# Gate and up products by one level of Strassen's scheme, and a down projection in two parts

## The chip, the cores and the metric

The kernel runs on one core of a Trainium2 chip. The metric is the device time of one execution in microseconds, as the median of several runs.

## The reference

One encoder layer on 512 tokens with 2048 features. The attention part (two groups of eight heads, and an output projection) stands ahead of the change and is not touched. What the change concerns is the feed-forward part:

```python
h2 = rms_norm(x, norm2_g) * (1 + sc2[:, None]) + sh2[:, None]
ff = (silu(h2 @ w_gate) * (h2 @ w_up)) @ w_down     # 2048 -> 5632 -> 2048
x = x + g2[:, None] * ff
return rms_norm(x, final_g)
```

## The kernel before, in words

Everything lies with features on the 128 partitions and the 512 tokens in columns. X is 16 tiles of 128x512; the normed input h2 stands as two fp32r parts, H_hi and H_lo (its rounded value and the rest), of 16 tiles each. Each weight is brought in as fp32 into one of four `raw` slots (SP's queue, `load`), copied by ScalarE to its rounded part W_hi (`split` at L705) and subtracted by VectorE to its rest W_lo (`split` at L1040). A product of two such pairs takes three matmuls of 512 columns: hi by hi, hi by lo, lo by hi (`tile`, L435 to L437).

A "piece" is eight weight tiles of 128x128 (1024 columns of W_hi, 512 KB). One gate/up step f makes 128 of the 5632 rows of F: two pieces of w_gate into bank Pb[0], two of w_up into Pb[1], 96 matmuls; ScalarE takes silu of Pb[0] to `gate` (L1005), VectorE multiplies by Pb[1] to `ftile` (L1524), and the pair F_hi, F_lo is made of it at once (L1009, L1526). There are 44 such steps, in four chunks of FC = 11. After each chunk a down part runs over the 16 tiles of X: two pieces of six and five tiles of w_down by the chunk's 11 tiles of F into Tb[0] or Tb[1], then `update_x` (L1429) adds the result to X. In the last chunk GpSimd sums squares of X behind the updates; then the column norm and the output follow.

The order of each engine is written out by hand. The semaphores that matter: `lo_done` counts finished low parts of weights (TensorE waits for it at each piece, SP reloads a raw slot by it), `used` counts pieces that TensorE has finished (ScalarE waits for it before it overwrites a part of W_hi; there are two parts, so a split can be one piece ahead), `gated`, `f_made`, `f_hi` and `mlp_ready` order the steps around F, `x_new` counts updates of X.

Of the kernel before, what the change touches and what calls it, by code (L numbers as in the profile page):

```python
# [20 lines left out]
F32 = mybir.dt.float32  # L21
# [4 lines left out]
P = 128  # L26
# [15 lines left out]
DK = (6, 5)  # L42
EPS = 1e-6
# [18 lines left out]
CP = 4 * FC + 2 * KT  # L62
# [11 lines left out]
def layer(nc, x, c, w_ada, b_ada, norm1_g, w_first, w_in, rpb, na_g, lam_p, sub_g, t5, w_out, norm2_g, w_gu, w_down,  # L74
          final_g, out):
    ctx = ExitStack()
    with ctx:
# [9 lines left out]

        H_hi = sb("H_hi", KT * S, F32R)
# [9 lines left out]
        W2_lo = nc.alloc_sbuf_tensor_at("W2_lo", [P, PW], F32R, offset=raw_at + (RAW_B + 1) * PW * 4)  # L98
        sq = sb("sq", 2 * S)
# [26 lines left out]
        F_hi = nc.alloc_sbuf_tensor_at("F_hi", [P, FC * S], F32R, offset=overlay)  # L126
        F_lo = nc.alloc_sbuf_tensor_at("F_lo", [P, FC * S], F32R, offset=overlay + FC * S * 4)
# [22 lines left out]
        t5_d = nc.dram_tensor("t5_d", [NAH, 1024], F32, kind="Internal")  # L150
        keys_d = nc.dram_tensor("keys_d", [NK, P, S], F32, kind="Internal")
# [53 lines left out]
        gated, f_made, f_hi = sem("gated"), sem("f_made"), sem("f_hi")  # L205
        dve_passed, pool_passed = sem("dve_passed"), sem("pool_passed")
# [5 lines left out]
        def w_parts(slot):  # L212

            if slot < 2:
                return W_hi[:, slot * PW:slot * PW + PW], W_lo[:, slot * PW:slot * PW + PW]
            return W2_hi[:, :], W2_lo[:, :]

# [53 lines left out]
        def _(sp):  # L271
# [135 lines left out]
            def mlp_loads(cc, f0):  # L407
                n0 = CP * cc + MLP0
                with sp.Fori(f0, FC) as f:
                    for j in range(4):  # L410
                        sp.wait_ge(lo_done, n0 + 4 * f + (j - 3))
                        load(j, w_gu[bass.ds(cc * (4 * FC) + 4 * f + j, 1)].rearrange("a p n -> (a p) n"), PW)
                with sp.Fori(0, KT // 2) as m:
                    for j in range(4):
                        sp.wait_ge(lo_done, n0 + 4 * m + (4 * FC + j - 3))
                        src = w_down[bass.ds(cc * KT + 2 * m + j // 2, 1)].rearrange("a p n -> (a p) n")
                        k0 = DK[0] * P * (j % 2)
                        load(j, src[:, k0:k0 + DK[j % 2] * P], DK[j % 2] * P)

            mlp_loads(0, 1)  # L420
            with sp.Fori(1, CH) as cc:
                mlp_loads(cc, 0)
# [7 lines left out]
        def _(pe):  # L430
# [242 lines left out]
            def chunk(cc, peel):  # L673
                n0 = CP * cc + MLP0
                f0 = 0
                if peel:
                    pair(n0, Pb, lambda k: pe.wait_ge(mlp_ready, k + 1))
                    f0 = 1
                with pe.Fori(f0, FC) as f:
                    for g in gate_up(n0, f):  # L680

                        pe.wait_ge(f_made if g else gated, cc * FC + f)
                with pe.Fori(0, KT // 2) as i:
                    for b in range(2):
                        m = 2 * i + b
                        pe.wait_ge(x_new, cc * KT + m + (KT - 1))
                        for h in range(2):
                            pe.wait_ge(mlp_ready, cc * FC + (KT + (DK[0] if h == 0 else FC)))
                            piece(n0 + 2 * m + (4 * FC + h), h, Tb[b], F_hi, F_lo,
                                  range(DK[0] * h, DK[0] * h + DK[h]), FC - 1)  # L690

            chunk(0, True)
            with pe.Fori(1, CH) as cc:
                chunk(cc, False)
# [4 lines left out]
        def _(act):  # L699
# [53 lines left out]
            def col_root(n):  # L753

                act.activation(root_warm[:, :], eps[:, :], ACT.Sqrt)
                act.wait_ge(x_new, KT if n == 3 else KT * (CH + 1))
# [228 lines left out]
            def mlp_group(cc, q):  # L985

                return (CP // 4) * cc + q + (NH + KT // 2)

            def split_gu(cc, f, j, slot_free=2):
                split(CP * cc + MLP0 + 4 * f + j, j % 2, j, landings(j, mlp_group(cc, f)), slot_free=slot_free)  # L990

            def split_down(cc, i, j):
                split(CP * cc + MLP0 + 4 * i + (4 * FC + j), j % 2, j, landings(j, mlp_group(cc, i + FC)), DK[j % 2] * P)

            def gate_up(cc, f, nxt):
                n = CP * cc + MLP0 + 4 * f
                pair = isinstance(f, int) and f == 0
                if not pair:
                    split_gu(cc, f, 1)
                    split_gu(cc, f, 2)  # L1000
                    split_gu(cc, f, 3)
                else:
                    nxt()
                act.wait_ge(used, n + (3 if pair else 2))
                act.activation(gate, Pb[0][:, :], ACT.Silu).then_inc(gated, 1)  # L1005
                if not pair:
                    nxt()
                act.wait_ge(f_made, cc * FC + f + 1)
                act.activation(F_hi[:, bass.ds(f * S, S)], ftile, ACT.Copy).then_inc(f_hi, 1)  # L1009

            def down(cc, i, nxt):
                for j in range(1, 4):
                    split_down(cc, i, j)
                if nxt:
                    nxt()

            def chunk(cc, last_one, f0=0):
                if f0:
                    gate_up(cc, 0, lambda: split_gu(cc, 1, 0, 4))
                with act.Fori(f0, FC - 1) as f:  # L1020
                    gate_up(cc, f, lambda: split_gu(cc, f + 1, 0))
                gate_up(cc, FC - 1, lambda: split_down(cc, 0, 0))
                with act.Fori(0, KT // 2 - 1) as i:
                    down(cc, i, lambda: split_down(cc, i + 1, 0))
                down(cc, KT // 2 - 1, None if last_one else lambda: split_gu(cc + 1, 0, 0))

            chunk(0, False, 1)
            with act.Fori(1, CH - 1) as cc:
                chunk(cc, False)
            chunk(CH - 1, True)  # L1030
# [4 lines left out]
        def _(dve):  # L1035
# [478 lines left out]
            def gate_up(cc, f, last_one):  # L1514
                n = CP * cc + MLP0 + 4 * f
                t = cc * FC + f
                if not (isinstance(f, int) and f == 0):
                    for j in range(1, 4):
                        split(n + j, j % 2, j)
                split(n + 4, 0, 0, DK[0] * P if last_one else PW)  # L1520
                dve.wait_ge(gated, t + 1)
                dve.wait_ge(used, n + 4)
                dve.wait_ge(mlp_ready, t + KT)
# [5 lines left out]
            def down(cc, i, nxt):  # L1529
# [5 lines left out]
                if nxt:  # L1535
                    split(n + 4, 0, 0, nxt)
                update_x(2 * i + 1, Tb[1], 5 * KT, n + 4)

            def chunk(cc, last_one, f0=0):
                if f0:  # L1540
                    gate_up(cc, 0, False)
# [194 lines left out]
```

## Time and profile before

| | us |
|---|---|
| median of 3 runs | 2379.63 (2378.16 to 2379.69) |
| profiled execution, its own time | 2379.1 |
| span of its profile | 2377.4 |
| attention part, up to the first gate matmuls | about 922 |
| feed-forward part (gate, up, down) | about 922 to 2357 |
| norm and output at the end | 2357 to 2377 |

In the profile L435 stands for line 435 of the kernel. PE is TensorE's matmul stream and PEld its weight loads, DVE is VectorE, ACT ScalarE, POOL GpSimd, SP the queue that issues most DMAs. A group names what is written and read (P<-H_hi,W_hi), the shape, the count, the busy time, the mean of one record in ns and the idle time ahead of it with its releaser. Matmul records overlap: the time of one is longer than the distance between two.

### The profile page before, as it was taken

To read this page: it belongs to the slowest core of one execution; us is meant where nothing else is said; L and a number is where in the kernel's file an instruction comes from. 1 tells how busy PE (TensorE), PEld (TensorE's weight loads), DVE (VectorE), ACT (ScalarE), POOL (GpSimd) and SP (SyncE) were. 2 spreads that over 40 slices of the span, in tenths; PEclk is the share of its full clock that TensorE was granted. 3 is DMA by queue.
4 is the path that set the end of the run, shared out by engine and by line. 5 is a ranking of instruction groups with operands and counts; after the bars stand their busy time and mean duration, and the time that the engine had idled before them with its cause. 6 is when DMAs were issued, how large, how long until landed. Compare 5 with 4: busy or idle time off the path is not lost.

```text
span 2377.4 us, 29120 instructions
## 1 busy us (share of the span) xinstructions
PE 2318.9 (98%) x10280; PEld 1883.5 (79%) x10280; DVE 1162.3 (49%) x1590; ACT 693.5 (29%) x978; POOL 236.0 (10%) x211
## 2 busy tenths in 40 slices
PE   7999999999999998999999999999999999999997
PEld 4878888766777886888888888888888888888885
DVE  6877777776767897222333222333222233222234
ACT  4234333444444114222222222222222222222221
POOL 4012333100004330000000000000000000000032
PEclk9999999999999998999999999999999999999998
DMA  9896766433435882222233322233222233222233
GB/s 335 271 358 171 201 196 197 165 108 128 170 109 210 324 289 71 97 97 97 82 97 106 103 95 94 84 96 109 97 97 97 82 96 113 97 97 88 87 97 107
DMA packets 120058, 333.75 MB, mean 140 GB/s; under 512 B 11897, under 2 KB 36617, under 8 KB 119505
## 3 DMA queue, kind: packets, MB, share of 16 engines
q1 hardware_dynamic: 115282, 318.03, 39.7%
q0 software_dynamic: 3728, 15.01, 2.7%
q8 instruction: 21, 0.34, 0.1%
q10 hardware_dynamic: 1008, 0.21, 0.0%
q14 instruction: 19, 0.16, 0.0%
HBM read 325.55 MB, written 7.65 MB: 140 GB/s over the span
## 4 chain that ended last, share of the span: by engine, by line
PE 92%; DVE 4%; DMA 2%; ACT 1%; POOL 1%; issue 1%; DVEq 0%; ACTq 0%; POOLq 0%
PE P L435 19%; PE P L437 19%; PE P L436 19%; PE T L435 9%; PE T L437 9%; PE T L436 9%; DMA att<-in_w_ada 1%; PE T L498 1%; PE S L480 1%; DVE W_lo L1040 1%; PE O L510 1%; PE O L511 1%; PE S L481 1%; PE O L512 1%; PE S L482 1%
## 5 line engine op out<-in xcount | busy, mean ns | idle before, releaser
L435 PE MATMUL P<-H_hi,W_hi 128*128 128x512 f32 x2112 | 840.1, 398 | 20.8 <-POOL ident L1594 10.8
L1040 DVE TENSOR_TENSOR W_lo<-raw,W_hi 128x1024 fp32r<-128x1024 f32 (+2 forms) x416 | 473.6, 1138 | 726.0 <-ACT W_hi L705 722.6
L437 PE MATMUL P<-H_hi,W_lo 128*128 128x512 f32 x2112 | 825.4, 391 | 0.0
L436 PE MATMUL P<-H_lo,W_hi 128*128 128x512 f32 x2112 | 825.0, 391 | 0.0
L705 ACT ACTIVATE W_hi<-raw 128x1024 fp32r<-128x1024 f32 (+2 forms) x416 | 406.2, 977 | 1056.8 <-PE P L437 568.4
L435 PEld LDWEIGHTS P<-H_hi,W_hi 128*128 128x128 f32 x2112 | 398.0, 188 | 117.8 <-issue 18.3
L437 PEld LDWEIGHTS P<-H_hi,W_lo 128*128 128x128 f32 x2112 | 397.9, 188 | 84.4
L436 PEld LDWEIGHTS P<-H_lo,W_hi 128*128 128x128 f32 x2112 | 398.5, 189 | 80.5 <-issue 1.9
L435 PE MATMUL T<-F_hi,W_hi 128*128 128x512 f32 x704 | 273.9, 389 | 0.0
L436 PE MATMUL T<-F_lo,W_hi 128*128 128x512 f32 x704 | 273.9, 389 | 0.0
L437 PE MATMUL T<-F_hi,W_lo 128*128 128x512 f32 x704 | 273.9, 389 | 0.0
L1642 POOL TENSOR_TENSOR sq<-X 128x512 f32 (+1 forms) x38 | 62.3, 1639 | 1540.0 <-DVE X L1429 1489.6
L437 PEld LDWEIGHTS T<-F_hi,W_lo 128*128 128x128 f32 x704 | 132.2, 188 | 27.5
L435 PEld LDWEIGHTS T<-F_hi,W_hi 128*128 128x128 f32 x704 | 132.2, 188 | 27.4
L436 PEld LDWEIGHTS T<-F_lo,W_hi 128*128 128x128 f32 x704 | 132.2, 188 | 27.3
L1429 DVE SCALAR_TENSOR_TENSOR X<-T,mod,X 128x512 f32 (+1 forms) x78 | 58.6, 751 | 129.7 <-PE T L437 129.2
L1049 DVE CUSTOM_DVE_ANT_0 adar<-adar,csb 128x1024 f32<-128x1024 f32 x72 | 97.2, 1364 | 33.7 <-DMA adar<-in_w_ada 33.7
L1524 DVE TENSOR_TENSOR gf<-gf,P 128x512 f32<-128x512 f32 x44 | 30.3, 689 | 145.4 <-PE P L437 145.4
L435 PE MATMUL T<-H_hi,W_hi 128*128 128x512 f32 x256 | 99.8, 390 | 1.1 <-DVE W_lo L1040 0.7
L437 PE MATMUL T<-H_hi,W_lo 128*128 128x512 f32 x256 | 99.6, 389 | 0.0
L436 PE MATMUL T<-H_lo,W_hi 128*128 128x512 f32 x256 | 99.6, 389 | 0.0
L1009 ACT ACTIVATE F_hi<-gf 128x512 f32 (+1 forms) x44 | 27.8, 632 | 231.2 <-DVE gf L1524 231.2
(167 smaller groups left out, 1645.6 us busy)
## 6 DMA issues: line engine op xcount, KB each, us to landing
raw<-in_w_gu SPq DMA_DIRECT2D x176, 512.0 KB, 3.2
raw<-in_w_in SPq DMA_DIRECT2D x72, 512.0 KB, 4.3
adar<-in_w_ada SPq DMA_DIRECT2D x72, 512.0 KB, 4.3
att<-in_w_ada SPq DMA_DIRECT2D x32, 1024.0 KB, 10.6
att<-in_w_ada SPq DMA_DIRECT2D x56, 512.0 KB, 4.8
raw<-in_w_down SPq DMA_DIRECT2D x64, 384.0 KB, 3.0
raw<-in_w_down SPq DMA_DIRECT2D x64, 320.0 KB, 2.9
raw<-in_w_out SPq DMA_DIRECT2D x32, 512.0 KB, 4.9
```

The costliest lines, as they stand in the source:

```text
L435: pe.matmul(bank[:, :], wh, xh, start=start, stop=False)
L436: pe.matmul(bank[:, :], wh, xl, start=False, stop=False)
L437: return pe.matmul(bank[:, :], wl, xh, start=False, stop=stop)
L480: pe.matmul(Sb[t % 2][:, :], qh[r, cols], kh[r, :], start=True, stop=False)
L481: pe.matmul(Sb[t % 2][:, :], qh[r, cols], kl[r, :], start=False, stop=False)
L705: act.activation(w_parts(slot)[0][:, 0:cols], raw[:, raw_slot * PW:raw_slot * PW + cols], ACT.Copy).then_inc(hi_done, 1)
L1009: act.activation(F_hi[:, bass.ds(f * S, S)], ftile, ACT.Copy).then_inc(f_hi, 1)
L1040: dve.tensor_tensor(lo[:, 0:cols], raw[:, raw_slot * PW:raw_slot * PW + cols], hi[:, 0:cols].bitcast(F32), ALU.subtract).then_inc(lo_done, 1)
L1049: dve.tensor_tensor_reduce(wt, wt, csb[:, half * 1024:half * 1024 + 1024], 1.0, 0.0, ALU.mult, ALU.add, st[:, acc:acc + 1]).then_inc(count ...
L1429: dve.scalar_tensor_tensor(xm, bank[:, :], mod[:, bass.ds(m + g0, 1)], xm, ALU.mult, ALU.add)\
L1524: dve.tensor_tensor(ftile, gate, Pb[1][:, :], ALU.mult).then_inc(f_made, 1)
L1642: pool.tensor_tensor(sq[:, S:2 * S], xk, xk, ALU.mult).then_inc(pool_sq, 1)
```

## The change

Of the 44 gate/up steps the first NPL = 4 stay as they are. In the other 40 the product of the 256x2048 weight block (gate and up rows of one step) and the 2048x512 input is taken as a 2x2 by 2x2 block product: the weights are A11, A12 (gate, first and second half of the features) and A21, A22 (up), the input is B11, B12, B21, B22 (two halves of the features by two blocks of HS = 256 tokens). One level of Strassen's scheme in Winograd's form makes seven products ("forms") where there were eight:

- input sums, made once during steps 1 to 3 by VectorE with their high parts by ScalarE (`make_t`, `t_high_half`, `t_low`): T1 = B12 - B11, T3 = B22 - B12, T2 = B22 - T1, T4 = B21 - T2, as hi and lo pairs;
- weight sums, made in each set by VectorE in the raw slots (`add_raw`, four of 128x1024);
- seven forms of eight tiles, each split to high and low as pieces were, each of 24 matmuls with 256 columns, in five banks beside the two of before; form 5 accumulates on form 0's bank, after ScalarE has copied form 0 to `p1s`;
- the results put together by VectorE with five operations of 256 columns (u2, u3, u4 and both halves of ftile) and `c_12`; silu in two halves (`silu_11`, `silu_12`), and one product of 512 columns (`f_product`).

The places for parts of weights are W_hi/W_lo and the columns of H_hi/H_lo that hold B12, which is not needed once the T's are made. F is no longer split as it is made: GpSimd's queue stores each `ftile` to device memory (`store_f`), and loads runs of tiles back (`load_f`, F_RUNS) into the places of T1 to T3 and of H, where ScalarE and VectorE split them (`f_high`, `f_low`). The down projection runs in CD = 2 parts of 22 tiles of F instead of four of 11, two tiles of X at a time (`down_pair`) in alternating banks; its pieces keep six and five tiles. TensorE waits for single tiles of F (`f_ready`) in the first pair of each part.

The diff, cut to its core:

```diff
-            def gate_up(n0, f):
-                for g in range(2):
-                    yield g
-                    for h in range(2):
-                        piece(n0 + 4 * f + (2 * g + h), h, Pb[g], H_hi, H_lo, half_kts(h), KT - 1)
...
+            def form(f, i, bank, rhs, start=True, reopen=False):
+                pe.wait_ge(lo_done, form_no(f, i + 1))
+                wh, wl = form_parts(FORM_SLOT[i])
+                out = bank[:, 0:HS]
+                for j in range(HALF):
+                    hi, lo = [w[:, j // 2, (j % 2) * P:(j % 2) * P + P] for w in (wh, wl)]
+                    xh, xl = rhs[j]
+                    pe.matmul(out, hi, xh, start=start and j == 0, stop=False, skip_group_check=reopen)
+                    pe.matmul(out, hi, xl, start=False, stop=False, skip_group_check=reopen)
+                    mm = pe.matmul(out, lo, xh, start=False, stop=j == HALF - 1, skip_group_check=reopen)
+                mm.then_inc(used, 1)
+
+            def product_set(f, first=False):
+                pe.wait_ge(gated, NPL) if first else pe.wait_ge(gate_a, f - NPL)
+                form(f, 0, Pb[0], B11, reopen=True)
+                if first:
+                    pe.wait_ge(f_made, NPL)
+                    pe.wait_ge(t_lo, 4 * HALF)
+                else:
+                    pe.wait_ge(u_made, 5 * f - 5 * NPL)
+                form(f, 1, Pb[1], T4c)
+                form(f, 2, Sb[0], T3c)
+                form(f, 3, Sb[1], T1c)
+                form(f, 4, Tb[0], T2c)
+                pe.wait_ge(p1_kept, f - (NPL - 1))
+                form(f, 5, Pb[0], B21, start=False, reopen=True)
+                if not first:
+                    pe.wait_ge(c12_made, f - NPL)
+                form(f, 6, Tb[1], B22)
...
+            def down_pair(c, i, banks, banks_free, f_wait=False, by_row=False):
+                for q in range(8):
+                    p, b = down_piece(q, by_row)
+                    if p == 0:
+                        banks_free(b)
+                    t0 = FD * c + (0, DK[0], FC, FC + DK[0])[p]
+                    n = down_no(c, i, q)
+                    pe.wait_ge(lo_done, n + 1)
+                    wh, wl = w_parts(q % 2)
+                    for j in range(DK[p % 2]):
+                        t = t0 + j
+                        if f_wait and b == 0:
+                            pe.wait_ge(f_ready, t + 1)
...
+            def product_set(f, first=False):
+                if not first:
+                    split_loaded(f, 0, form_no(f, -2))
+                    silu_11(f - 1)
+                split_loaded(f, 1, form_no(f, 0 if first else -1))
+                split_form(f, 2, summed, 4 * f + (1 - 4 * NPL), form_no(f, 0))
+                if not first:
+                    silu_12(f - 1)
+                split_form(f, 3, summed, 4 * f + (2 - 4 * NPL), form_no(f, 0))
+                act.wait_ge(used, form_no(f, 1))
+                if not first:
+                    act.wait_ge(u_made, 5 * f - (5 * NPL + 4))
+                act.activation(p1s, Pb[0][:, 0:HS], ACT.Copy).then_inc(p1_kept, 1)
+                split_form(f, 4, summed, 4 * f + (3 - 4 * NPL), form_no(f, 1))
+                split_loaded(f, 5, form_no(f, 2))
+                split_form(f, 6, summed, 4 * f + (4 - 4 * NPL), form_no(f, 3))
...
+            def product_set(f, first=False):
+                g5 = 5 * f - 5 * NPL
+                if not first:
+                    split_form(f, 0)
+                dve.wait_ge(raw_in[2], landings(2, f + GRP0))
+                add_raw(0, 0, 2)
+                split_form(f, 1)
+                if not first:
+                    c_12(f - 1)
+                add_raw(2, 2, 3)
+                if not first:
+                    f_product(f - 1)
+                split_form(f, 2)
+                add_raw(3, 3, 0)
+                split_form(f, 3)
+                split_form(f, 4)
+                split_form(f, 5)
+                add_raw(1, 1, 3)
+                split_form(f, 6)
+                dve.wait_ge(used, form_no(f, 5))
+                dve.wait_ge(p1_kept, f - (NPL - 1))
+                dve.tensor_tensor(u2, Tb[0][:, 0:HS], p1s, ALU.subtract).then_inc(u_made, 1)
...
+            def c_12(f):
+                dve.wait_ge(used, form_no(f, 7))
+                dve.wait_ge(u_made, 5 * f - 5 * (NPL - 1))
+                dve.tensor_tensor(u4, Tb[1][:, 0:HS], u4, ALU.subtract).then_inc(c12_made, 1)
...
+            def silu_11(f):
+                act.wait_ge(used, form_no(f, 6))
...
+            split_down(0, 0, 0, slot_free=3)
+            silu_11(FT - 1)
+            f_high(0, 1, 2, 3)
+            split_down(0, 0, 1, slot_free=3)
+            f_high(4, 5)
+            silu_12(FT - 1)
+            f_high(6, 7)
...
+            def load_f(r, n_used):
+                t0, t1 = F_RUNS[r]
+                pool.wait_ge(used, n_used)
+                pool.wait_ge(f_stored, 16 * t1)
...
+            for r, n in enumerate((DOWN0 - 4, DOWN0 - 3, DOWN0 - 3, DOWN0 - 2, DOWN0, DOWN0, DOWN0)):
+                load_f(r, n)
...
+            for r, q in ((7, 2), (8, 2), (9, 4), (10, 4), (11, 6), (12, 6)):
+                load_f(r, down_no(0, HALF - 1, q))
```

## Rows read from the trace of the kernel before

**Rows 1.** The page: busy shares of the span, and granted clock in 40 slices.

```profile
PE 2318.9 (98%) x10280; PEld 1883.5 (79%) x10280; DVE 1162.3 (49%) x1590; ACT 693.5 (29%) x978; POOL 236.0 (10%) x211
...
PEclk9999999999999998999999999999999999999998
```

**Rows 2.** The page's chain of work that ended last.

```profile
PE 92%; DVE 4%; DMA 2%; ACT 1%; POOL 1%; issue 1%; DVEq 0%; ACTq 0%; POOLq 0%
PE P L435 19%; PE P L437 19%; PE P L436 19%; PE T L435 9%; PE T L437 9%; PE T L436 9%; DMA att<-in_w_ada 1%; PE T L498 1%; PE S L480 1%; DVE W_lo L1040 1%; PE O L510 1%; PE O L511 1%; PE S L481 1%; PE O L512 1%; PE S L482 1%
```

**Rows 3.** Grouped lines of 945 to 2367 us (columns as on the page).

```profile
L435 PE MATMUL P<-H_hi,W_hi 128*128 128x512 f32 x1373 | 534.1, 389 | 0.0
...
L1040 DVE TENSOR_TENSOR W_lo<-raw,W_hi 128x1024 fp32r<-128x1024 f32 (+2 forms) x299 | 323.3, 1081 | 691.1 <-ACT W_hi L705 688.1
L705 ACT ACTIVATE W_hi<-raw 128x1024 fp32r<-128x1024 f32 (+2 forms) x299 | 282.7, 945 | 849.2 <-PE P L437 484.1 <-PE T L437 365.2
...
L435 PEld LDWEIGHTS P<-H_hi,W_hi 128*128 128x128 f32 x1372 | 257.6, 188 | 53.4
```

**Rows 4.** Timeline, gate/up step: start, duration, engine, group.

```profile
1400.15 0.39 PE L436 MATMUL P<-H_lo,W_hi 128*128 128x512 f32 x1
...
1400.37 0.39 PE L437 MATMUL P<-H_hi,W_lo 128*128 128x512 f32 x1
1400.38 0.19 PEld L435 LDWEIGHTS P<-H_hi,W_hi 128*128 128x128 f32 x1
...
1401.28 0.39 PE L435 MATMUL P<-H_hi,W_hi 128*128 128x512 f32 x1
```

**Rows 5.** Timeline of VectorE, then of ScalarE, around one product.

```profile
1412.77 0.69 DVE L1526 TENSOR_TENSOR F_lo<-gf,F_hi 128x512 f32 x1 [0.92 <-ACT F_hi L1009]
1413.64 1.23 DVE L1040 TENSOR_TENSOR W_lo<-raw,W_hi 128x1024 fp32r<-128x1024 f32 x1 [0.18 <-ACT W_hi L705]
...
1411.98 0.63 ACT L1009 ACTIVATE F_hi<-gf 128x512 f32 x1 [5.36 <-DVE gf L1524]
1412.55 1.06 ACT L705 ACTIVATE W_hi<-raw 128x1024 fp32r<-128x1024 f32 x1
...
1433.74 0.63 ACT L1009 ACTIVATE F_hi<-gf 128x512 f32 x1 [5.36 <-DVE gf L1524]
```

**Rows 6.** Timeline of TensorE at 31 us, where the granted clock is 0.50.

```profile
31.41 0.63 PE L435 MATMUL P<-H_hi,W_hi 128*128 128x512 f32 x1
31.84 0.63 PE L436 MATMUL P<-H_lo,W_hi 128*128 128x512 f32 x1
```

**Rows 7.** Timeline of TensorE around four transposes in the attention part.

```profile
212.76 0.60 PE L489 MATMUL M<-ident,att 128*128 128x128 f32 x4
...
213.09 0.19 PEld L435 LDWEIGHTS P<-H_hi,W_hi 128*128 128x128 f32 x1
...
213.19 0.19 PEld L436 LDWEIGHTS P<-H_lo,W_hi 128*128 128x128 f32 x1
```

**Rows 8.** Timeline of VectorE in the attention part, operations without a wait.

```profile
417.81 0.68 DVE L1075 CUSTOM_DVE_ANT_0 att<-S,att 128x512 f32<-128x512 f32 x1
...
418.42 1.22 DVE L1040 TENSOR_TENSOR W_lo<-raw,W_hi 128x1024 fp32r<-128x1024 f32 x1
419.55 0.68 DVE L1075 CUSTOM_DVE_ANT_0 att<-S,att 128x512 f32<-128x512 f32 x1
```

**Rows 9.** DMA issues: count, KB each, median us from issue to landing.

```profile
raw<-in_w_gu SPq DMA_DIRECT2D x176, 512.0 KB, 3.2
...
X<-in_x POOLq DMA_DIRECT2D x4, 1024.0 KB, 5.9
...
keys_d<-adar POOLq DMA_DIRECT2D x13, 256.0 KB, 6.4
```

**Rows 10.** Timeline at the end of the last down part.

```profile
2357.56 0.75 DVE L1429 SCALAR_TENSOR_TENSOR X<-T,mod,X 128x512 f32<-128x512 f32 x1 [5.82 <-PE T L437]
```

**Rows 11.** Waits of TensorE's weight loads: us in total, times, longest.

```profile
PEld P L435 <- issue: 18.3, 41, 3.2
```

More of the change, by code:

```diff
@@ L42 @@
 DK = (6, 5)
+HS = S // 2
+NPL = 4
+FS = FT - NPL
+NF = 7
+CD = 2
+FD = FT // CD
 EPS = 1e-6
@@ L405, in _ @@
                 load(j, w_gu[PAIR_SRC[j]], PW)
[L407 to L418, printed above, removed]
@@ L692, in _, with column @@
-            chunk(0, True)
-            with pe.Fori(1, CH) as cc:
-                chunk(cc, False)
+                        piece(4 * f + (MLP0 + 2 * g + h), h, Pb[g], H_hi, H_lo, half_kts(h), KT - 1)
+            def column(src, k0, c0, step):
+                return [[a[:, (k0 + j) * step + c0:(k0 + j) * step + c0 + HS] for a in src[0:2]] for j in range(HALF)]
+            H = (H_hi, H_lo)
+            B11, B21, B22 = column(H, 0, 0, S), column(H, HALF, 0, S), column(H, HALF, HS, S)
+            T1c, T2c, T3c, T4c = [column(t, 0, 0, HS) for t in (T1, T2, T3, T4)]
@@ L983, in _ @@
                     split_out(KT // 2, 3, 2)
[L985 to L1001, printed above, removed]
-                else:
[L1003 to L1025, printed above, removed]
@@ new lines, in _ @@
+            for f in range(1, NPL):
+                for j in range(1, 4):
+                    split_gu(f, j)
+                    if 3 * f - 4 + j < HALF:
+                        t_high_half(3 * f - 4 + j)
+                act.wait_ge(used, MLP0 + 4 * f + 2)
+                act.wait_ge(f_made, f)
+                act.activation(gate, Pb[0][:, :], ACT.Silu).then_inc(gated, 1)
+                if f < NPL - 1:
+                    split_gu(f + 1, 0)
+                else:
+                    split_loaded(NPL, 0, STR0 - 1)
@@ new lines, in _, with f_high, split_down @@
+            product_set(NPL, True)
+            with act.Fori(NPL + 1, FT) as f:
+                product_set(f)
+            def f_high(*ts):
+                for t in ts:
+                    f_landed(act, t)
+                    hi, _, full = f_home(t)
+                    act.activation(hi, full, ACT.Copy).then_inc(f_hi, 1)
+            def split_down(c, i, q, by_row=False, slot_free=2):
+                if isinstance(q, int) and q == 8:
+                    c, i, q = (c, i + 1, 0) if not isinstance(i, int) or i < HALF - 1 else (c + 1, 0, 0)
+                split(down_no(c, i, q), q % 2, q % 4, 16 * (2 * i + (8 * 2 * c + FT + GRP0 + q // 4)) + landings(q % 4, 0),
+                      down_cols(q, by_row), slot_free)
@@ new lines, in down_pair @@
+            def down_pair(c, i, by_row=False, end=9):
+                for q in range(1, end):
+                    split_down(c, i, q, by_row)
+            with act.Fori(2, HALF - 1) as i:
+                down_pair(0, i)
+            down_pair(0, HALF - 1)
+            for q, ts in ((1, range(28, 34)), (2, ()), (3, range(34, 39)), (4, ()), (5, range(39, 44)), (6, ()), (7, ()),
+                          (8, ())):
+                split_down(1, 0, q)
+                f_high(*ts)
+            with act.Fori(1, HALF - 1) as i:
+                down_pair(1, i)
@@ L1511, in _ @@
                     split(MLP0 + 3, 2, 3)
[L1514 to L1523, printed above, removed]
-                dve.tensor_tensor(ftile, gate, Pb[1][:, :], ALU.mult).then_inc(f_made, 1)
-                dve.wait_ge(f_hi, t + 1)
-                dve.tensor_tensor(F_lo[:, bass.ds(f * S, S)], ftile, F_hi[:, bass.ds(f * S, S)].bitcast(F32),
-                                  ALU.subtract).then_inc(mlp_ready, 1)
```

334 lines of the change are left out of this document (283 added, 51 removed).

## Prediction

> **What bounds the kernel now.** I read the page's busy shares first, then its chain, then the gate/up stretch in the grouped lines and the timeline. TensorE is busy for 98% of the span, its weight loads for 79%, VectorE for 49%, and the granted clock is at its upper level, 2.4 GHz, through the whole feed-forward part [rows 1]. The chain that ended last is 92% TensorE, 57% of the span of it in the three matmul lines that write P [rows 2]. So the question of every edit is what it does to the stream of matmuls; work of ScalarE, VectorE and the DMA queues counts only where a matmul comes to wait for it. In the feed-forward part none does: the matmul groups have no idle time ahead of them, while VectorE sat 691 us and ScalarE 849 us waiting, nearly all for TensorE [rows 3].
>
> A busy sum misleads here, because a matmul's record (389 ns) is longer than the distance between two. The timeline gives the distance: from the start at 1400.15 to the one at 1401.28 there are five distances, 0.226 each [rows 4]. One gate/up step, read from one F_hi activation to the next (1411.98 to 1433.74), is 21.76 us [rows 5]; it holds 4 pieces x 8 tiles x 3 = 96 matmuls, and 21.76 / 96 = 0.2267. At the lower clock level (granted 0.50, so 1.2 GHz) the same matmuls start 0.43 apart [rows 6], which is 512 columns at one a cycle; at 2.4 GHz that alone would be 0.2133, so 0.0133 is lost with each.
>
> **What goes: 40 steps of products.** 40 x 21.76 = 870.4 us.
>
> **What comes: 40 sets of seven products.** A set is 7 forms x 8 tiles x 3 = 168 matmuls of 256 columns, against 192 halves before; each has its own weight load, where before there were 96. So the saving is not 1/8 by itself: a column half costs the same only if a 256-column matmul costs half of 0.2267. The break-even is 21.76 / 168 = 0.1295 us for each matmul. The trace has no fp32r matmul of 256 columns, so I bound it.
> - Below: half of the 512-column distance, 0.1133, if the lost 0.0133 is a share of the columns.
> - Middle: 0.1067 of stream plus the whole 0.0133, if it is lost once for each matmul: 0.1200.
> - By the load: the record of a weight load is 0.188 [rows 3]. If that is the time for which the load path is held, and loads can't overlap, matmuls come no closer than 0.188.
>
> Which of them holds is seen where matmuls are short. A load starts with the matmul before its own (1400.37 and 1400.38 [rows 4]). Of four transposes of 128 columns, each with a load of its own, the first starts at 212.76, and with the fourth, at 213.09, starts the load behind them: three distances in 0.33, 0.11 each. The next load, of the projection's kind as the last, starts at 213.19, 0.10 to 0.11 on, though each is recorded with 0.19 [rows 7]. So the record includes latency, and the load path accepts the next load after about 0.11. That lies under 0.12: 256 columns would just cover it. It lies over 0.1067, so a load is now nearly as long as the stream over it; there is no room left.
>
> The Trainium skill (TensorE: Matmul & The Clock Gate, "LDWEIGHTS (loading the stationary operand)") puts a load at its columns over 1.2 GHz, 107 ns for 128. The 0.11 between loads agrees and the record of 0.188 doesn't; by the rule the load hides and the change gains, by the record the sum would come out hundreds of microseconds slower.
>
> Between 0.1133 and 0.1200 I take 0.1200: that the loss comes with the instruction, by its switch of weights, seems likelier than with columns, and a load at 0.11 plus a few ns of switching gives nearly the same. A set is 168 x 0.1200 = 20.16 us; 40 make 806.4. Difference: **-64.0 us**.
>
> **Do VectorE and ScalarE keep up with a set?** From starts of neighbours without a wait, VectorE gives its place up 1.13 after a 128x1024 operation and 0.61 after one of 512 [rows 8]; for 256 columns I extrapolate to 0.61 - (1.13 - 0.61) / 2 = 0.35. A set has 7 low parts and 4 sums of 1024 (12.4), the F product (0.6) and six operations of 256 (2.1): 15.1 us of 20.16. The upper bound takes durations (1.23 and 0.69, so 0.42 for 256 columns) and the 0.18 that stands ahead of an operation that has just been released [rows 5] for all: 15.5 + 0.9 + 3.6 = 20.0, just under a set's length. ScalarE has 7 x 1.06 and three of 256 (about 0.4, from 0.63 for 512) [rows 5]: 8.6 us. Neither is the bound, but VectorE's order has to be walked. Count from the end of form 4; a form takes 2.88.
> - Its five combinations end at 2.0, form 0's low part at 3.2; needed at 5.76.
> - Sum 1 ends at 4.3, form 1's low part at 5.6 (its high part waits for the end of form 5 at 2.88 and silu_11, and ends at 4.3); needed at 8.64.
> - c_12 waits for form 6 (5.76) and ends at 6.2, sum 2 at 7.3. ScalarE copies form 2 from 5.8 to 6.8, then silu_12 to 7.2. F product to 7.9, form 2's low part to 9.1; needed at 11.52.
> - Sum 3 10.2, form 3 11.3 (needed 14.4), form 4 12.5 (17.3), form 5 13.8, sum 4 15.0, form 6 17.2 (23.0). VectorE then waits for form 4's end at 20.16.
>
> The smallest margins are 2.5 us, at forms 0 and 2. At the upper bound they shrink to about nothing, without a loss. The raw pieces are reloaded from 10.2, 11.3, 15.0 and 17.2 on, and a 512 KB load lands 3.2 us later [rows 9], each ahead of its turn. Traffic is 4 x 512 + 256 KB in 20.16 us, about 115 GB/s, where one such load alone moves 160 (512 KB in 3.2 us). The store of F (6.4 us for 256 KB from this queue [rows 9]) has from 7.9 to about 21. Cost: 0.
>
> **Before the sets.** Steps 1 to 3 keep their matmuls. VectorE gets eight times two operations of 512 and eight of 256, 4.0 us, some 0.3 more for waits on itself; three of those in a step with four splits and a product: 3 x 4.3 + 4 x 1.13 + 0.6 = 18.0 of 21.76. Each piece lasts 5.44 and asks 4.3 + 1.13 = 5.4 of VectorE, with a margin made in the fourth: 0. In the first set form 1 needs a high part that waits for the last piece (1.1), the product, a sum and the low part: 0.7 + 1.1 + 1.2 = 3.0 against 2.88. **+0.1**, up to 2.
>
> **Down.** 16 rows x 44 tiles x 3 = 2112 matmuls, as before, at 0.2267. In two parts there are 32 updates of X where there were 64, all behind a bank that TensorE has left: 0. The F parts are no longer made beside each step (0.63 and 0.69 a tile [rows 5]) but as tiles arrive. Count from the end of the last form. The first run is asked for when three forms are done, at -11.5, and needs 5.9 us (1 MB from this queue [rows 9]); ScalarE, held by silu_11 to -2.4, has four high parts by -0.2, VectorE the fourth low part at 0.4, where TensorE wants it at 2.0. Tiles 4 and 5: run two, asked for at -8.6; after the split of piece 1 they are ready at 1.8 and 2.4, wanted at 2.7 and 3.4. Piece 1 uses the same tiles, so to 8.2 there is time for c_12, silu_12, the last F and the split of piece 2, which ends near 6.4. The other tiles have 3.4 or 4.1 us of slack for each two or three. Runs for the second part start 21.7, 14.9 and 6.8 us ahead of it. **+1**, from 0 to 5, since three runs of 1 MB land together with weights. The end (2357.5 to the last record, 20 us) has the same steps [rows 10].
>
> **The sum.** -64.0 + 0.1 + 1 + 1 for waits not seen = -62, against the profiled execution's 2379.1 (span 2377.4): 2317. The median stands 0.5 above it: **2318 us**.
>
> **Rivals.**
> - *The loss goes with the columns*: 0.1133, a set of 19.04, -109: **2272**. For it: half the columns, half the time, and loads fit under it at 0.11 by 3 ns. Against it: two limits within 3 ns seldom both hide.
> - *The heads of the forms stall.* A set has seven heads where a step had four, each with a wait computed by the sequencer, and a stall that 0.2267 hid no longer hides under 0.12. In the attention part TensorE's loads of L435 found 41 times that nothing but issue held them, 18.3 us in all, 0.45 each [rows 11]. At 0.1 a head it is +0.7 a set, +28: **2346**; from 0.23 a head (64 / 40 / 7) the gain is gone, at 0.45 it is +126. Against it: 8 instructions went out in 0.44 for the transposes, 0.055 each, where a set at 0.12 allows 0.060, and the four heads of a step show no gap now [rows 3]. The Trainium skill (same page, "Wait — 56ns, not 53.3ns?") names about 62 ns of sequencer time for a MATMUL if hardware decode is off; if a load costs as much, a pair takes 0.124 and the sum would come to some 2343 by the page; no row settles it.
> - *The weight load is the bound* (the other side): place, every matmul of a form; price, 168 x 0.188 = 31.6 a set, +9.8 x 40 = +393: **2771**. It decides from 0.1295. For it: the 0.188 record, and two streams that both fill their time, which the trace never has for long. Against: loads 0.11 apart [rows 7].
> - *VectorE's order is the bound*: if each high part is made only after the operation ahead of it on VectorE, 7 x (1.06 + 0.18) [rows 5] come on top of 15.1: 23.8 a set, +81: **2460**. Against: only forms 4 and 6 have that order in the walk.
>
> **Chances and range.** Forecast 0.62; columns 0.12; heads of forms or other short stalls, still faster, 0.13; load 0.06; VectorE or long stalls at heads, slower, 0.05; no change 0.02, a sum of part losses. A difference of 0.2% (4.8 us) is about what a measurement tells from none. Faster 0.87, same 0.02, slower 0.11. The range goes from 2271 (all of the columns' case) to 2350, 0.8 us a set over the forecast, which takes in 0.1 us a head; the slow cases, 0.11, stay outside.
>
> **What would show it.** 256-column matmuls start 0.120 apart and an F product follows the last by 20.2; the weight loads' busy share nears 100%, with distance 0.12, not 0.19. VectorE waits 2 to 5 us a set. TensorE has no idle time at first matmuls of forms but a little in the first set and at the first down pieces. Down stays at 0.2267. I am wrong if the distance is above 0.1295, or if each set has a wait for W_lo or u.

## The result and the profile after

The kernel with the change takes 2316.31 us (median of 4 runs, 2315.2 to 2317.39), the one before on the same chip 2379.66. The ratio is 0.9737, with an interval of 0.9726 to 0.9749: faster by 63 us. The forecast was 2318. The span of the profile went from 2377.4 to 2315.5 us.

The page of the kernel after: busy shares, then slices of TensorE's loads and of the granted clock.

```profile
PE 2256.2 (97%) x13160; PEld 1968.7 (85%) x13160; DVE 1578.2 (68%) x2158; ACT 850.6 (37%) x1210; POOL 264.1 (11%) x268
...
PEld 5878788777777887799999999999999888888885
...
PEclk9999999999999998999999999999999999999998
```

TensorE stays the engine that is always busy and its clock is as in [rows 1]; VectorE went from 49% to 68%, and the weight loads fill 9 tenths or more of the slices with product sets. The grouped lines of the stretch of the sets (1010 to 1840 us), the counterpart of [rows 3]:

```profile
L805 PE MATMUL S<-T_hi,H_hi 128*128 128x256 f32 x640 | 181.1, 283 | 0.0
...
L1172 ACT ACTIVATE W_hi<-raw 128x1024 fp32r<-128x1024 f32 x159 | 168.1, 1058 | 213.3 <-PE T L807 155.3 <-DVE raw L1783 48.6 <-PE P L554 4.4
L1780 DVE TENSOR_TENSOR H_lo<-raw,H_hi 128x1024 fp32r<-128x1024 f32 x120 | 146.6, 1222 | 48.1 <-ACT H_hi L1172 48.1
...
L805 PEld LDWEIGHTS S<-T_hi,H_hi 128*128 128x128 f32 x640 | 122.9, 192 | 0.0
```

No idle time ahead of these matmuls and loads (the only wait in the whole stretch is one of 0.3 in the first set). A load is still recorded with 0.19 us, and a matmul of 256 columns with 0.283. The timeline has their distance:

```profile
1399.72 0.28 PE L807 MATMUL S<-T_hi,H_lo 128*128 128x256 f32 x1
1399.84 0.28 PE L805 MATMUL S<-T_hi,H_hi 128*128 128x256 f32 x1
1399.96 0.28 PE L806 MATMUL S<-T_lo,H_hi 128*128 128x256 f32 x1
1400.08 0.28 PE L807 MATMUL S<-T_hi,H_lo 128*128 128x256 f32 x1
1400.20 0.28 PE L805 MATMUL S<-T_hi,H_hi 128*128 128x256 f32 x1
```

0.12 each, against 0.2267 for 512 columns [rows 4]. VectorE's timeline through one set, from the combination behind form 4 to the next one:

```profile
1407.69 0.43 DVE L1834 TENSOR_TENSOR tail<-T,tail 128x256 f32<-128x256 f32 x1 [2.84 <-PE T L807]
...
1409.48 1.22 DVE L1780 TENSOR_TENSOR W_lo<-raw,W_hi 128x1024 fp32r<-128x1024 f32 x1
1410.62 1.22 DVE L1783 TENSOR_TENSOR raw<-raw 128x1024 f32<-128x1024 f32 x1
1411.84 1.23 DVE L1780 TENSOR_TENSOR W_lo<-raw,W_hi 128x1024 fp32r<-128x1024 f32 x1
1413.46 0.42 DVE L1806 TENSOR_TENSOR tail<-T,tail 128x256 f32<-128x256 f32 x1 [0.39 <-PE T L807]
...
1415.54 1.22 DVE L1780 TENSOR_TENSOR H_lo<-raw,H_hi 128x1024 fp32r<-128x1024 f32 x1
...
1423.78 1.23 DVE L1780 TENSOR_TENSOR H_lo<-raw,H_hi 128x1024 fp32r<-128x1024 f32 x1 [1.20 <-ACT H_hi L1172]
1427.85 0.42 DVE L1834 TENSOR_TENSOR tail<-T,tail 128x256 f32<-128x256 f32 x1 [2.84 <-PE T L807]
```

A set is 1427.85 - 1407.69 = 20.16 us. The walk counted from the end of form 4, where form 5 starts. TensorE's timeline has that start:

```profile
1407.40 0.28 PE L805 MATMUL P<-H_hi,W_hi 128*128 128x256 f32 x1
```

The first combination starts 0.29 behind it. Counted from 1407.40, form 0's low part ends at 3.3 (1410.70; walked: 3.2), form 1's at 5.7 (5.6), form 2's at 9.4 (9.1), form 6's at 17.6 (17.2). The smallest margins are 5.76 - 3.30 = 2.46 us at form 0 and 11.52 - 9.36 = 2.16 at form 2. What is left of the set shows as a wait for TensorE of 2.84.

**Where the time came from.** The first product of F and the last update of X, in the timelines of VectorE after, stand against 942.86 before and [rows 10]:

```profile
944.04 0.69 DVE L1788 TENSOR_TENSOR gf<-gf,P 128x512 f32<-128x512 f32 x1 [2.90 <-PE P L554]
...
2295.30 0.75 DVE L1665 SCALAR_TENSOR_TENSOR X<-T,mod,X 128x512 f32<-128x512 f32 x1 [5.05 <-PE T L850]
```

Between the two lie 1351.26 us where 1414.70 lay: -63.4. The part ahead of it took 1.2 more and the end 0.4 more, so the span lost 61.9. The 1.2 is within what profiles differ by in the attention part, which the change leaves alone: in those of the twelve kernels of this case the first product of F starts between 941.3 and 944.3. The first set's wait, in TensorE's timeline, accounts for what the -63.4 lacks of -64:

```profile
1012.04 0.28 PE L806 MATMUL P<-H_lo,W_hi 128*128 128x256 f32 x1
1012.16 0.28 PE L807 MATMUL P<-H_hi,W_lo 128*128 128x256 f32 x1
1012.77 0.35 PE L805 MATMUL P<-T_hi,W_hi 128*128 128x256 f32 x1 [0.33 <-DVE W_lo L1780]
1012.97 0.28 PE L806 MATMUL P<-T_lo,W_hi 128*128 128x256 f32 x1
```

From 1012.16 to 1012.97 are 0.81 where two distances are 0.24: 0.57 lost, so 40 x 1.6 - 0.57 = 63.4.

### The profile page after: what moved, and what is told of

Same layout as the page of the kernel before. It is cut to its first block, busy times and chain, and to the rows that moved or that the text cites. A ratio compares the mean times of both kernels' runs of the same rounds, so it can differ in the third digit from the quotient of the medians.

```text
span 2315.5 us, 36235 instructions
## 1 busy us (share of the span) xinstructions
PE 2256.2 (97%) x13160; PEld 1968.7 (85%) x13160; DVE 1578.2 (68%) x2158; ACT 850.6 (37%) x1210; POOL 264.1 (11%) x268
## 4 chain that ended last, share of the span: by engine, by line
PE 91%; DVE 4%; DMA 2%; ACT 1%; POOL 1%; issue 1%; DVEq 0%; SPq 0%; ACTq 0%; POOLq 0%
PE P L552 7%; PE P L554 7%; PE P L553 7%; PE P L805 5%; PE P L806 5%; PE P L807 5%; PE S L849 3%; PE T L849 3%; PE T L848 3%; PE S L850 3%; PE S L848 3%; PE T L850 3%; PE T L807 3%; PE T L806 3%; PE T L805 3%; PE S L807 3%
## 5 line engine op out<-in xcount | busy, mean ns | idle before, releaser
L1276 DVE TENSOR_TENSOR W_lo<-raw,W_hi 128x1024 fp32r<-128x1024 f32 (+2 forms) x256 | 283.5, 1107 | 331.7 <-ACT W_hi L879 330.9
L552 PE MATMUL P<-H_hi,W_hi 128*128 128x512 f32 x832 | 341.5, 410 | 20.9 <-POOL ident L1948 9.2
L554 PE MATMUL P<-H_hi,W_lo 128*128 128x512 f32 x832 | 326.9, 393 | 0.0
L553 PE MATMUL P<-H_lo,W_hi 128*128 128x512 f32 x832 | 326.4, 392 | 0.0
L1780 DVE TENSOR_TENSOR W_lo<-raw,W_hi 128x1024 fp32r<-128x1024 f32 x160 | 194.4, 1224 | 3.3 <-ACT W_hi L1172 2.9
L1783 DVE TENSOR_TENSOR raw<-raw 128x1024 f32<-128x1024 f32 x160 | 195.0, 1219 | 0.0
L554 PEld LDWEIGHTS P<-H_hi,W_lo 128*128 128x128 f32 x832 | 157.1, 189 | 34.3
L805 PE MATMUL S<-T_hi,H_hi 128*128 128x256 f32 x640 | 181.1, 283 | 0.0
L806 PE MATMUL S<-T_lo,H_hi 128*128 128x256 f32 x640 | 181.1, 283 | 0.0
L807 PE MATMUL S<-T_hi,H_lo 128*128 128x256 f32 x640 | 181.1, 283 | 0.0
```

What stands on the lines that cost most here:

```text
L552: pe.matmul(bank[:, :], wh, xh, start=start, stop=False)
L553: pe.matmul(bank[:, :], wh, xl, start=False, stop=False)
L554: return pe.matmul(bank[:, :], wl, xh, start=False, stop=stop)
L805: pe.matmul(out, hi, xh, start=start and j == 0, stop=False, skip_group_check=reopen)
L806: pe.matmul(out, hi, xl, start=False, stop=False, skip_group_check=reopen)
L807: mm = pe.matmul(out, lo, xh, start=False, stop=j == HALF - 1, skip_group_check=reopen)
```

## The experiments

The questions, in order: what sets 0.12 for a matmul of 256 columns; whether the sets hold the whole gain; how near VectorE's order is to a stall; whether the reload of F costs; and whether the 0.0133 us that is lost with each matmul can be won back. "The kernel after" has 2316.31 us. Beside these runs the kernel before had medians of 2378.04 to 2379.18, where it had 2379.66 beside the kernel after, so differences of a us or two between medians are not told from none; a period read in the timeline is sharper. The kernels with fewer columns leave out a part of each product.

### Half the columns

```diff
-                out = bank[:, 0:HS]
+                out = bank[:, 0:128]
...
-                    xh, xl = rhs[j]
+                    xh, xl = [x[:, 0:128] for x in rhs[j]]
```

> Every matmul of a form takes only the first 128 of its 256 columns; the other half of each product is left out, so the output is not the reference's. The prediction's reasons: the lost 0.0133 us comes with the instruction, and the load path accepts the next load after 0.11. Stream and loss would be 0.053 + 0.013 = 0.067, so the loads set the distance: 0.109 to 0.110, a set of 18.4 us, 1.8 x 40 = 70 less than the changed kernel's 2316: 2246. Rival: a load and its switch take 0.120, and this, not the stream, set the distance of the 256-column matmuls: no change, 2316. Rival: loads are no limit at all: 0.067, then VectorE's 17 us of work and waits a set bound it, about 2190.

Measured: 2940.1 us, ratio 1.236 (1.2335 to 1.2385). The windows of this kernel (columns: busy time and count of PE, PEld, DVE, ACT and POOL, granted clock, DMA share, GB/s):

```profile
1005.00:1010.00 5.00, 4.55 (x33) 4.10 (x31) 2.98 (x4) 2.12 (x2) 0.54 (x1) 1.00 0.12 45
1010.00:1015.00 5.00, 4.88 (x30) 4.91 (x31) 5.00 (x5) 2.91 (x4) 0.00 (x0) 0.68 0.10 30
1400.00:1440.00 40.00, 40.00 (x189) 40.00 (x189) 19.41 (x22) 9.96 (x13) 1.08 (x2) 0.50 0.20 68
...
2445.00:2450.00 5.00, 5.00 (x24) 4.14 (x23) 3.54 (x6) 3.21 (x7) 0.00 (x0) 1.00 0.95 342
```

Its timeline of TensorE, at the upper clock level and later:

```profile
1008.94 0.28 PE L807 MATMUL P<-H_hi,W_lo 128*128 128x128 f32 x1
1009.05 0.28 PE L805 MATMUL P<-H_hi,W_hi 128*128 128x128 f32 x1
...
1399.71 0.41 PE L805 MATMUL P<-H_hi,W_hi 128*128 128x128 f32 x1
1399.92 0.41 PE L806 MATMUL P<-H_lo,W_hi 128*128 128x128 f32 x1
```

As long as the clock was granted whole, the matmuls started 0.11 apart, as expected of the loads: half the columns, and only a hundredth of a microsecond less than with 256. Then the granted clock went from 1.00 to 0.50 (1.2 GHz): in the first set, from 1011.87 on, the distance is 0.213 (40 us / 189 = 0.212), and a set takes 35.8 us. TensorE's only wait in the sets is one of 0.57 us, at 1010.12, shortly before; but the two kernels of the next section have one of 0.5 at the same place, and the granted clock stayed at 1.00 there. The clock came back only in the down projection, behind a few matmuls of 512 columns (0.427 apart up to 2441.52, 0.23 from 2441.95 on). So the expected 2246 us was missed by 694 for a cause that no theory had, and only the distance at the upper level answers the question. A second size was wanted.

### 240 columns, and 192

The same edit with 240 and with 192.

> Every matmul of a form takes the first 240 of its 256 columns; 16 columns of each product are left out, so the output is not the reference's. The prediction's reasons (loss once for each instruction, loads at 0.11 under it): 0.1000 + 0.0133 = 0.1133, a set of 19.04, -45: 2271. Rival (load and switch take 0.120): 2316. A loss that goes with the columns is excluded already by 0.120 at 256.

> The forms take 192 of each block's 256 columns, so that a fourth of every gate and up product of the 40 sets is left out. By the columns a matmul would take 0.12 - 64 x 0.000417 = 0.0933 us, less than the 0.11 that the weight loads took with 128 columns at the upper clock: 168 x 0.11 = 18.5 us for a set, and 2316 - 40 x 1.7 = 2250 us, if the granted clock stays up. Rival: what made the granted clock fall with 128 columns is that the loads set the distance, and it falls here too: 168 x 0.213 = 35.8 us for a set, and 2940 us, as with 128 columns.

Measured: 2261.85 us (0.9509, 0.949 to 0.9528) and 2259.92 (0.9503, 0.9485 to 0.952). VectorE's timeline has the period of a set, with 240 columns first and then with 192:

```profile
1399.22 0.42 DVE L1834 TENSOR_TENSOR tail<-T,tail 128x256 f32<-128x256 f32 x1 [1.94 <-PE T L807]
...
1418.04 0.42 DVE L1834 TENSOR_TENSOR tail<-T,tail 128x256 f32<-128x256 f32 x1 [1.94 <-PE T L807]
```

```profile
1397.83 0.42 DVE L1834 TENSOR_TENSOR tail<-T,tail 128x256 f32<-128x256 f32 x1 [1.90 <-PE T L807]
...
1416.59 0.42 DVE L1834 TENSOR_TENSOR tail<-T,tail 128x256 f32<-128x256 f32 x1 [1.90 <-PE T L807]
```

18.82 / 168 = 0.1120 us a matmul and 18.76 / 168 = 0.1117. From 240 to 192 columns a fifth of the stream goes and next to nothing of the time, and 128 columns had the same distance at the upper clock level (1007.05 to 1009.28, 20 distances of 0.1115): there the weight load sets the distance, at 0.112. From 256 to 240 the distance falls by 0.008, where 16 columns at 2.4 GHz are 0.0067: so at 256 it is the columns and what is lost with them that count, not the load. The load theory of 0.12 is out. With it the strict form of "0.0133 is lost with each matmul" is out too, since it would leave 0.1133 at 240 columns. The Trainium skill (TensorE: Matmul & The Clock Gate, "LDWEIGHTS (loading the stationary operand)") puts a load at its columns over 1.2 GHz, 107 ns for 128: near the 0.112 here, while the record says 0.19. It doesn't give the 0.213 that the run with 128 columns had at a granted clock of 0.50. With 192 columns the granted clock stayed 1.00 from 1010 to 1840 us, so that loads set the distance is not what made it fall with 128.

### One form twice, and half the sets

```diff
-                for j in range(HALF):
+                for j in [*range(HALF), *(range(HALF) if i == 4 else ())]:
```

> Form 4's 24 matmuls are issued twice (the first 24 are overwritten by the second, the output stays), as many matmuls as eight products of 256 columns would take. If TensorE's stream is the only bound: 24 x 0.120 = 2.88 a set, +115.2: 2431.5. That is above the kernel before, 2379.7: halving the columns costs more than the gain of one product of eight, and only seven make it pay. Rival (VectorE's order holds a part of each set): under +100, since a longer set gives it time.

Measured: 2430.8 us (1.0219, 1.0199 to 1.0239). Form 4's 24 matmuls once more in each of 40 sets add 114.5 us by the medians, 0.1193 each, and by VectorE's timeline a set takes 23.04 (1417.84 to 1440.88) in place of 20.16, 0.1200 each: so the time follows TensorE's matmuls at their distance, and nothing else in a set had room to hide them. With the matmuls of an eighth form the gain is a loss.

```diff
-NPL = 4
+NPL = 24
```

> 24 steps stay plain and 20 are taken as seven products; F through device memory and the two-part down projection stay as in the changed kernel. If the whole gain is 1.60 us a set, it is 20 x 1.60 = 32.0 above the changed kernel: 2348.3, and drawn on to no set at all 2380.3, so the rest of the change (F stored and loaded, down in two parts, transition) costs 0.6. Rival: the down part in two parts gains or costs some 5 us of its own, and the slope differs: 2343 or 2353.

Measured: 2348.06 us (0.987, 0.9854 to 0.9887). Twenty sets fewer cost 31.75 us, 1.59 a set, where the prediction's 21.76 - 20.16 is 1.60. Carried on to no sets at all, 2316.31 + 2 x 31.75 = 2379.8, the time before: the way over device memory and the down projection in two parts neither cost nor give anything that this can tell. A us of error in either median is one or two in the 2379.8, so some 3 us either way could hide in it; the 5 of the rival could not.

### More work for VectorE, ahead of form 0's low part and elsewhere

```diff
+                for n in range(5):
+                    if not (first and n == 0):
+                        dve.wait_ge(extra, 5 * f - 5 * NPL + n)
+                    dve.tensor_tensor(rstd[:, :], X[:, 0:S], X[:, S:2 * S], ALU.add).then_inc(extra, 1)
                 if not first:
                     split_form(f, 0)
```

> Five more VectorE operations of 512 columns (about 0.69 us each with the wait on the one before, 3.45 in all) stand in each set between the five combinations and form 0's low part. By the walk, form 0's low part ends at 3.05 + 3.45 = 6.5 where it is needed at 5.76: a set grows by about 0.8, 32 in all: 2348. Rival: only VectorE's total counts (15.7 of work, 1.2 of wait for the last form's high part, 3.45 new: 20.35 of 20.16): +8, 2324.

Measured: 2369.37 us (0.9956, 0.994 to 0.9973), 53.1 over the kernel after, where 32 was expected. VectorE's timeline of this kernel, then TensorE's, then TensorE's waits in the stretch of the sets:

```profile
1412.69 0.42 DVE L1839 TENSOR_TENSOR tail<-T,tail 128x256 f32<-128x256 f32 x1 [1.18 <-PE T L808]
...
1414.48 3.59 DVE L1819 TENSOR_TENSOR rstd<-X 128x512 f32<-128x512 f32 x5
1417.99 1.22 DVE L1781 TENSOR_TENSOR W_lo<-raw,W_hi 128x1024 fp32r<-128x1024 f32 x1
```

```profile
1418.04 0.28 PE L808 MATMUL T<-H_hi,H_lo 128*128 128x256 f32 x1
1419.26 0.39 PE L806 MATMUL P<-H_hi,W_hi 128*128 128x256 f32 x1 [0.94 <-DVE W_lo L1781]
1419.48 0.28 PE L807 MATMUL P<-H_lo,W_hi 128*128 128x256 f32 x1
```

```profile
PE P L806 <- DVE W_lo L1781: 39.7, 39, 3.8
```

The stall is where the walk put it: the low part of form 0 ends at 1419.21, and TensorE, which could have gone on at 1418.04 + 0.12 = 1418.16, starts at 1419.26. Its second matmul follows after 0.22 in place of 0.12, so a set loses 1.10 + 0.10 = 1.2 us. The expectation had 0.8. The five operations are not the reason: they took 3.51 (1414.48 to 1417.99) where 3.45 was expected. It counted form 0's low part from the start of the combination and its need from form 5's start, 0.29 earlier; with that, 3.30 + 3.51 - 5.76 = 1.05 is the stall, and 0.05 for the release and 0.10 at the second matmul come on top. 39 sets make 47 of the 53 us; the longest wait, 3.8, is the first set's, at form 1's head, which the expectation left out.

Three such operations in place of five:

```diff
-                for n in range(5):
+                for n in range(3):
```

> Three of these operations (2.07 us) ahead of form 0's low part. By the walk it ends at 5.1, needed at 5.76, and the round of VectorE is 19.0 of 20.16: no change, 2316. Rival (any added work there is paid): +83.

Measured: 2319.97 us (0.9745, 0.9729 to 0.9762). The waits of TensorE in the stretch of the sets:

```profile
PE P L806 <- DVE W_lo L1781: 2.4, 1, 2.4
PE S L849 <- DVE T_lo L1856: 0.9, 1, 0.9
```

The first set's wait (2.4 where the kernel after has 0.3) and the first down pieces' (0.9) are 3.0 of the 3.7 us; 39 sets have no wait. So the margin at form 0's head is real and ends between three and five operations, as the 2.46 us above say: three take 2.1, five 3.5.

The same five operations behind form 6's low part, where VectorE waits for TensorE anyway:

```diff
                 split_form(f, 6)
+                for n in range(5):
...
                 dve.wait_ge(used, form_no(f, 5))
```

> The same five operations stand behind form 6's low part, where VectorE waits 2.84 us for form 4's end. By the walk and by the total: 17.35 + 3.45 = 20.8 against 20.16, so the combinations come 0.6 late, form 0's low part at 3.7 (needed 5.76), but VectorE's own round is 20.35 at least: +0.2 a set, +8, 2324, up to +25 if its wait for the last form's high part moves along. Rival (any added work on VectorE is paid): +3.45 a set, +138.

Measured: 2315.77 us (0.9729, 0.9713 to 0.9745), no difference, where 8 us were expected. VectorE's timeline:

```profile
1402.11 3.59 DVE L1836 TENSOR_TENSOR rstd<-X 128x512 f32<-128x512 f32 x5
1405.62 0.41 DVE L1839 TENSOR_TENSOR tail<-T,tail 128x256 f32<-128x256 f32 x1
...
1425.78 0.42 DVE L1839 TENSOR_TENSOR tail<-T,tail 128x256 f32<-128x256 f32 x1
```

A set is 20.16 as before. The five (3.5 in all) fill the 2.84 that VectorE waited, and the combinations come some 0.6 later, for which form 0's low part has room. VectorE waits for TensorE no more, so its round just fits into the set; the expectation had it 0.2 longer. 53 us or none: what VectorE's 68% don't say, its order does.

### F asked for late

```diff
-            for r, n in enumerate((DOWN0 - 4, DOWN0 - 3, DOWN0 - 3, DOWN0 - 2, DOWN0, DOWN0, DOWN0)):
+            for r, n in enumerate((DOWN0,) * 7):
```

> All seven runs of F for the first part of the down projection are asked for only when the last form is done, instead of four of them up to 11.5 us ahead. The early ones are then not hidden: 1 MB takes 5.9 us, the first high and low part 1.2 more, and the next tiles are bound by the landing of runs: +7 to +9, 2324. Rival (transition is not on the path): +0.

Measured: 2325.06 us (0.9768, 0.9752 to 0.9785), 8.75 over the kernel after. TensorE's longest wait, of which the kernel after has none by this name:

```profile
PE S L848 <- DVE T_lo L1851: 7.6, 1, 7.6
```

So F's reload is hidden because it is asked for up to four forms early: the 11.5 us of lead that the prediction counted cover it.

### The high weights by both input parts in one matmul

If the loss goes mostly with the instruction, fewer and longer ones win it back. Forms 1, 2, 3, 4 and 6 take hi by (hi, lo) as one matmul of 512 columns into both halves of the bank; ScalarE and VectorE add the halves.

```diff
-                    pe.matmul(out, hi, xh, start=start and j == 0, stop=False, skip_group_check=reopen)
-                    pe.matmul(out, hi, xl, start=False, stop=False, skip_group_check=reopen)
-                    mm = pe.matmul(out, lo, xh, start=False, stop=j == HALF - 1, skip_group_check=reopen)
+                    if j:
+                        pe.matmul(out, lo, xh, start=False, stop=False, skip_group_check=True)
+                    mm = pe.matmul(bank[:, :], hi, both, start=j == 0, stop=j == HALF - 1)
+                    if j == 0:
+                        pe.matmul(out, lo, xh, start=False, stop=False, skip_group_check=True)
...
+                for k, (dst, bank) in enumerate(((w1, Pb[1]), (w2, Sb[0]), (w3, Sb[1]))):
+                    act.wait_ge(used, form_no(f, k + 2))
+                    act.activation(dst, bank[:, HS:S], ACT.Copy).then_inc(w_kept, 1)
```

> Forms 1, 2, 3, 4 and 6 multiply the high weights by both parts of the input in one matmul of 512 columns, into both halves of the bank, and the low weights by the high part in one of 256: 16 matmuls for 24. ScalarE copies the right halves of three banks out, VectorE adds the halves, five more operations of 256 elements in each set. The loss goes with the instruction (0.0133 us each: 512 columns 0.2267, 256 columns 0.12): each of these forms takes 8 x (0.2267 + 0.12) = 2.77 us for 2.88, a set 19.63 for 20.16, and the time is 2316 - 40 x 0.53 = 2295 us (2290 to 2299), if VectorE's longer order stays hidden: form 0's low part then ends about 4.2 us behind form 4's end, where 5.65 are left. Rival: a matmul that adds into half of the bank that the one before has just written waits for it, and nothing is won: 2316 or more. Second rival: the added operations of VectorE and ScalarE are late for form 0 or form 2: 40 x 0.1 us back for each 0.1, with TensorE's waits on VectorE in the trace.

Measured: 2299.66 us (0.967, 0.9657 to 0.9683), 16.7 under the kernel after and just above the expected 2290 to 2299. TensorE's timeline of this kernel, then VectorE's:

```profile
1401.34 0.40 PE L826 MATMUL T<-H_hi 128*128 128x512 f32 x1
1401.57 0.28 PE L828 MATMUL T<-H_hi 128*128 128x256 f32 x1
1401.69 0.28 PE L825 MATMUL T<-H_hi 128*128 128x256 f32 x1
1401.81 0.40 PE L826 MATMUL T<-H_hi 128*128 128x512 f32 x1
1402.05 0.28 PE L825 MATMUL T<-H_hi 128*128 128x256 f32 x1
1402.16 0.40 PE L826 MATMUL T<-H_hi 128*128 128x512 f32 x1
```

```profile
1398.76 0.42 DVE L1864 TENSOR_TENSOR tail<-T,tail 128x256 f32<-128x256 f32 x1 [1.10 <-PE T L826]
...
1418.55 0.43 DVE L1864 TENSOR_TENSOR tail<-T,tail 128x256 f32<-128x256 f32 x1 [1.16 <-PE T L826]
```

A set takes 19.78 (mean of 39; 19.79 between these two). Forms 0 and 5 have 48 matmuls of 0.12, 5.76, so a pair of the other five forms takes (19.78 - 5.76) / 40 = 0.3505, where 0.2267 + 0.12 = 0.3467 was expected. No wait of TensorE was added: the one in the sets is the first set's 0.3 again, so neither rival holds. The sets give 40 x 0.38 = 15.2 us, seven tenths of the expected 21; 1.3 of the 16.7 lie ahead of the first product of F, which starts at 942.7 in this profile and at 944.0 in that of the kernel after. Why the mixed pair costs 0.004 more than its parts stays open. It is the fastest kernel here that computes the whole product.

## Why the prediction was right

- **The distance of 256 columns** (0.1133, 0.1200 or 0.188; 0.1200 taken): 0.12 in the timeline, 20.16 a set, 0.1200 by the period with the doubled form. This one choice made the forecast: 168 x 40 matmuls put 45 us between the two lower values. Its reason, that the loss comes with the instruction, holds for most of it (512 and 256 columns both lose 0.0133, and longer matmuls won 0.38 / 40 = 0.0096 for each one that they spared), but not to the last nanosecond, by the run with 240 columns, which loses 0.0120 at most. What the loss consists of was not shown, and that 0.1200 was taken and not 0.1133 was a judgement that no row of before could settle.
- **Loads accept the next one after 0.11, record 0.19:** shown. The floor by itself is 0.112 with 192 and 240 columns, and the record stays at 0.19. The rival by the record, 2771, did not come, and the distance of a form's matmuls is 0.008 over that floor, as thin as the prediction said. That two limits within 3 ns seldom both hide, its argument against 2272, is shown by no run.
- **-64.0 for the sets:** 40 x 1.60 by the period, 1.59 by the run with half the sets.
- **VectorE keeps up, smallest margins 2.5 us at forms 0 and 2:** 2.5 and 2.2; the walk's times came within 0.1 us for forms 0 and 1 and 0.4 at the end of the round, and the runs with three and five operations put the end of the margin between 2.1 and 3.5. Its upper bound, that margins shrink to nothing, was too dark.
- **+0.1 for the first set, +1 for the way into down, +1 unseen:** 0.57 in the first set, at the place that the prediction named; 0 at the down part, where the last matmul of the forms starts at 1816.24 and the first of down at 1816.36. The unseen part was 1.2 ahead of the first product of F, within what profiles differ by there, and 0.4 at the end, which was not followed. The three together, 2.1 against 2.1, agree by luck: one term was five times too small, one came to nothing, and the third holds a difference between runs. In detail the run loads took 8.4 and 12.5 us to land where the prediction took 5.9, hidden by their lead.
- **Heads of forms stall (2346):** no idle time ahead of the forms but the first set's. Seven heads a set cost nothing measurable. Nor did a pair of load and matmul need the 0.124 that the prediction worked out for this rival: pairs ran at 0.112 with 240 and 192 columns. (Its time for 0.124 comes to 2345 by its own sum, not 2343: 168 x 0.004 x 40 = 27.)
- **VectorE's order as the bound (2460):** as counted, few forms have a high part that waits for VectorE just ahead of the low part; only form 6's makes VectorE wait, 1.20 a set, in time that VectorE had.

## What to carry to other kernels

A matmul's price is the distance between starts, not its record, and has a part for its columns and a part for itself: a scheme that halves the columns to save an eighth of the products pays the second part twice, and gains only while the new distance stays under its break-even (here 0.120 against 0.1295). The weight load behind each matmul sets a floor to that distance (here 0.112), however few the columns. Before such a change, look for the shortest matmuls in the trace and read how closely they and their loads follow one another. And walk the order of the engine that feeds the stream: the same five operations cost 53 us in one place and none in another.

## What the runs showed of the hardware that was not expected

- The granted clock fell from 1.00 to 0.50 when the matmuls had 128 columns and started 0.11 apart, and stayed there through the sets, some 1400 us in which TensorE had no gap; it came back behind the first matmuls of 512 columns. With 192 and 240 columns, 0.112 apart and with the same short wait in the first set, it stayed at 1.00. What makes the difference wasn't tried further. The distance of matmuls nearly doubled by it, and a cut of the columns by half made the kernel 24% slower than the one before.
- At the lower level the distance of those 128-column matmuls was 0.213, not 0.11. At the upper level that distance is the load's; if it is so here too, which one size can't show, the load goes with the clock: 111.7 ns x 2.4 GHz = 268 and 213.3 ns x 1.2 GHz = 256 granted cycles for 128 columns.
- The 0.0133 that a matmul of 512 columns loses shows at the upper level only: at the lower one they start 0.427 apart in the run with 128 columns (nine distances in 3.84), which is 512 / 1.2 GHz with nothing on top.
- The distance falls by 0.008 from 256 to 240 columns and by 0.0003 from 240 to 192: the load's floor is sharp.
